# Storing the expert result rows by an indirect DMA that leaves out unused rows

## What is computed

```python
def _hier_moe(h, w_rg, b_rg, w_re, b_re, w_gate, w_up, w_down):
    t = h.reshape(b * s, d)                       # 512 tokens x 1024
    g_logits = (t @ w_rg + b_rg)                  # 4 groups of 8 experts
    g_idx = jnp.argmax(g_logits, axis=-1)         # one group a token
    e_sel = ...                                   # the 8 expert logits of that group
    top_v, top_i = lax.top_k(e_sel, 2)            # two experts a token
    top_w = jax.nn.softmax(top_v, axis=-1) * g_w
    for gi in range(4):
        hg, hu = t @ w_gate[gi], t @ w_up[gi]     # 1024 -> 256, each expert
        act = jax.nn.silu(hg) * hu * combine
        out = out + act @ w_down[gi]              # 256 -> 1024
```

## Time and profile before

| | us |
|---|---|
| median of 3 runs (891.83 to 893.46) | 893.3 |
| the profiled execution, whole | 893.97 |
| its span, from first to last instruction | 892.2 |
| PE busy | 778.1 (87%) |
| DVE busy | 436.9 (49%) |
| ACT busy | 179.4 (20%) |
| POOL busy | 156.1 (18%) |

### The profile page before, as it was taken

How to read it: one execution, slowest core, us unless ns; L and a number is a source line. 1 busy time by engine, 2 the same in 40 slices (tenths; PEclk the granted TensorE clock), 3 DMA queues, 4 the chain that set the end, 5 groups by cost and what they waited for, 6 DMA issues and landing times.

```text
span 892.2 us, 9829 instructions
## 1 busy us (share of the span) xinstructions
PE 778.1 (87%) x3913; PEld 527.0 (59%) x3913; DVE 436.9 (49%) x743; ACT 179.4 (20%) x333; POOL 156.1 (18%) x74
## 2 busy tenths in 40 slices
PE   0399997799999999999999999999999989988700
PEld 0388786789887888544444688885554544544200
DVE  5999806455668888311135678362212220211138
ACT  4212323344232321000000110121111111111022
POOL 5734663220042221100000060000000000000042
PEclk9999998899999999999999999999999999999955
DMA  9523321111121132622110351807999999999562
GB/s 294 191 93 96 94 94 48 48 49 48 48 95 48 48 82 61 239 91 79 63 47 1 139 239 47 327 4 279 423 424 422 423 422 421 423 423 422 228 212 95
DMA packets 57860, 163.48 MB, mean 183 GB/s; under 512 B 14412, under 2 KB 37078, under 8 KB 45014
## 3 DMA queue, kind: packets, MB, share of 16 engines
q1 hardware_dynamic: 51744, 139.68, 41.2%
q0 software_dynamic: 3072, 12.63, 4.0%
q10 hardware_dynamic: 2998, 10.53, 2.9%
HBM read 148.15 MB, written 14.68 MB: 182 GB/s over the span
## 4 chain that ended last, share of the span: by engine, by line
PE 71%; DMA 15%; DVE 9%; issue 2%; ACT 1%; POOL 1%; SPq 1%; ACTq 0%; DVEq 0%; POOLq 0%
PE psum L744 24%; DMA ring<-in_w_exp_up_dram 11%; PE psum L1038 9%; PE psum L953 6%; PE psum L943 6%; PE psum L992 5%; PE psum L1053 3%; PE psum L934 3%; PE psum L1015 2%; DMA ring<-in_w_in_dram 2%; PE psum L1016 2%; DVE arena L1398 2%; PE psum L883 2%; DVE arena L1397 2%; PE psum L903 1%
## 5 line engine op out<-in xcount | busy, mean ns | idle before, releaser
L744 PE MATMUL psum<-ring_r 128*128 128x512 f32 (+1 forms) x768 | 213.3, 363 | 2.6 <-DVE arena L1569 1.3
L744 PEld LDWEIGHTS psum<-ring_r 128*128 128x128 f32 x768 | 139.4, 194 | 26.2 <-issue 2.4
L675 POOL TENSOR_TENSOR ring_r<-ring,ring_r 128x2048 fp32r<-128x2048 f32 x20 | 93.4, 4670 | 205.5 <-ACT ring_r L1109 205.5
L1038 PE MATMUL psum<-ring,arena 128*64 128x512 f32 x512 | 113.1, 594 | 11.5 <-DMA ring<-in_w_exp_up_dram 10.7
L1109 ACT COPY arena<-psum 128x512 f32<-128x512 f32 (+3 forms) x102 | 57.5, 582 | 290.8 <-PE psum L960 139.8
L744 PE MATMUL psum<-arena_r,ring_r 128*128 128x512 f32 x256 | 100.5, 392 | 0.0
L1038 PEld LDWEIGHTS psum<-ring,arena 128*64 128x64 f32 x512 | 40.2, 137 | 82.7 <-issue 81.8
L1824 DVE SCALAR_TENSOR_TENSOR arena<-arena,psum 128x256 f32<-128x256 f32 x16 | 9.9, 621 | 120.5 <-ACT arena L1291 120.5
L707 POOL DMA_INDIRECT ring<-y_rows,rowsU x8 | 9.1, 1132 | 328.5 <-ACT arena L1109 326.4
L1015 PE MATMUL psum<-arena_r 128*128 128x256 f32 x256 | 65.3, 293 | 0.0
L1016 PE MATMUL psum<-arena_r 128*128 128x256 f32 x256 | 62.5, 282 | 0.0
(11 more groups left out here) (242 smaller groups left out, 956.8 us busy)
## 6 DMA issues: line engine op xcount, KB each, us to landing
ring<-in_w_exp_gate_dram SPq DMA_DIRECT2D x32, 1024.0 KB, 17.3
ring<-in_w_exp_up_dram SPq DMA_DIRECT2D x32, 1024.0 KB, 19.5
ring<-in_w_exp_down_dram SPq DMA_DIRECT2D x32, 1024.0 KB, 19.4
ring<-in_w_in_dram SPq DMA_DIRECT2D x18, 1024.0 KB, 5.1
y_rows<-arena ACTq DMA_DIRECT2D x16, 512.0 KB, 8.0
y_rows<-arena POOLq DMA_DIRECT2D x4, 1024.0 KB, 7.2
ring<-in_w_out_ssd_dram SPq DMA_DIRECT2D x4, 1024.0 KB, 7.3
ring<-in_w_out_dram SPq DMA_DIRECT2D x4, 1024.0 KB, 11.1
```

What stands on the lines that cost most here:

```text
L675: g.tensor_tensor(lo, ring[:, SLOT_OF[seq]], hi.bitcast(F32), ALU.subtract).then_inc(s_w_lo, 1)
L744: t = mm(o, a, b, start=(first and j == 0), stop=(last and j == 2))
L1038: t = mm(psum[sides[half], parity, :], xgT[buf][:, k, c:c + CAP], ring[:, s:s + 2, k, :], start=(k == 0), stop=(k == KD - 1))
```

## The change

Three things are changed.

1. The store of a pair's results moves from ACT (direct DMA) to POOL, which issues an indirect DMA for each of the 16 pairs. It takes the row number of each partition from a column of `storeU`; a used row has its old number, an unused one a number beyond the buffer, and rows beyond the buffer are left out (`oob_is_err=False`). The further pairs in the loop keep ACT's direct store, with a wait for it behind.
2. DVE computes `storeU`: two small compares where the counts are, and three small operations after the last embedding tile. POOL makes two more small index tables.
3. All 3072 rows of `y_rows` are zeroed early, by twelve DMAs of 1 MB in place of four, at the same place.

```diff
-ZERO_DMAS = (ROWS - NE * CAP) // P // 2
+ZERO_DMAS = ROWS // P // 2
...
-            zview_y = y_dram[NE * CAP:ROWS].rearrange("(p r) n -> p r n", p=P)
+            zview_y = y_dram.rearrange("(p r) n -> p r n", p=P)
             for r in range(0, zview_y.shape[1], 2):
                 pool.dma_start(zview_y[:, r:r + 2, :], zt).then_inc(s_zeroed, 16)
...
+            g.iota(row_id, pattern=[[2 * CAP, PAIRS]], base=0, channel_multiplier=1,
+                   allow_small_or_imprecise_dtypes=True).then_inc(s_iota_c, 1)
+            g.iota(row_of, pattern=[[-CAP, 2]], base=0, channel_multiplier=1,
+                   allow_small_or_imprecise_dtypes=True).then_inc(s_iota_c, 1)
             pool.wait_ge(s_pe_yT, NT)
...
+            pool.wait_ge(s_store_ready, 1)
+            for p in range(PAIRS):
+                pool.wait_ge(s_y_act, p + 1)
+                pool.wait_ge(s_y_dve, p + 1)
+                g.indirect_dma_start(
+                    out=y_dram, out_offset=bass.IndirectOffsetOnAxis(ap=storeU[:, p:p + 1], axis=0), in_=eout[:, p % 2, :],
+                    in_offset=None, bounds_check=ROWS - 1, oob_is_err=False).then_inc(y_st[p % 2], 16)
             pool.wait_ge(s_rows_ready, 2)
             pool.wait_ge(s_blocks_stored, 1)
...
                 copy(eout[:, u % 2, 0:512], psum[:, 4, :]).then_inc(s_y_act, 1)
-                act.wait_ge(s_y_act, p + 1)
-                act.wait_ge(s_y_dve, p + 1)
-                act.dma_start(y_dram[bass.ds(p * 2 * CAP, 2 * CAP)], eout[:, u % 2, :]).then_inc(y_st[u % 2], 16)
...
-            act.wait_ge(y_st[0], pairs * 16 + 16 * (PAIRS // 2))
+            act.wait_ge(y_st[0], 16 * (PAIRS // 2))
             act.wait_ge(y_st[1], 16 * (PAIRS // 2))
...
+            dve.wait_ge(s_iota_c, 3)
+            for half in range(2):
+                q = slice(half * CAP, (half + 1) * CAP)
+                ins = v.tensor_tensor(store_f[q], count[q, half:NE:2], row_of[q, half:half + 1].broadcast_to([CAP, PAIRS]),
+                                      ALU.is_gt)
+                link(ins)
...
             for n in range(4 * NT - RANKS_AFTER, 4 * NT):
                 ple_out(n)
+            link(v.tensor_scalar(store_f, store_f, -float(4 * ROWS), float(4 * ROWS), ALU.mult, ALU.add))
+            link(v.tensor_tensor(store_f, store_f, row_id, ALU.add))
+            v.tensor_copy(storeU[:, :], store_f).then_inc(s_store_ready, 1)
             dve.wait_ge(s_pe_pl, 4 * NT)
             tokens_rows(1, 1, None, 1, 4 * CAP)
```

More of the change, by code:

```diff
@@ L109 @@
 RING = SLOTS * SLOT
-ARENA = 28600
+ARENA = 28512
 RANKS_AFTER = 2
@@ L356, in block_kernel @@
         sums = shaped(region(4 * NT), "p (i n) -> p i n", i=NT, n=4)
+        row_id = at(region(PAIRS), PAIRS)
+        row_of = at(region(2), 2)
+        store_f = at(region(PAIRS), PAIRS)
+        storeU = ctx.enter_context(nc.sbuf_tensor("storeU", [P, PAIRS], U32))
         rowsU = ctx.enter_context(nc.sbuf_tensor("rowsU", [P, 2 * NT], U32))
@@ L400, in block_kernel @@
         s_iota_c = sem("iota_c")
+        s_store_ready = sem("store_ready")
         s_hT_read = sem("hT_read")
@@ L409, in block_kernel @@
         s_mix_read = sem("mix_read")
+        s_more_stored = sem("more_stored")
         s_mix_ready = sem("mix_ready")
@@ L1328, in _ @@
                     act_copy(p, 0)
-                    out_copy(p, j * 16 + 16 * (PAIRS // 2), 0)
+                    out_copy(p, 16 * (PAIRS // 2), 0)
+                    act.wait_ge(s_y_act, p + 1)
+                    act.wait_ge(s_y_dve, p + 1)
+                    act.dma_start(y_dram[bass.ds(p * 2 * CAP, 2 * CAP)], eout[:, 0, :]).then_inc(s_more_stored, 16)
+                    act.wait_ge(s_more_stored, j * 16 + 16)
+                    copy(rv[10], rv[8])
                 act.nop()
-            act.wait_ge(y_st[0], pairs * 16 + 16 * (PAIRS // 2))
+            act.wait_ge(y_st[0], 16 * (PAIRS // 2))
             act.wait_ge(y_st[1], 16 * (PAIRS // 2))
@@ L1802, in h1_rest @@
                 v.tensor_tensor(h_lo[:, i], h1[:, i], h_hi[i].bitcast(F32), ALU.subtract).then_inc(s_h1_lo, 1)
-            dve.wait_ge(s_iota_c, 1)
             tokens_rows(0, 0, None, None, 4 * CAP)
@@ L1844, in _ @@
                     hidden(j + PAIRS, 0)
-                    out_half(j + PAIRS, j * 16 + 16 * (PAIRS // 2), 0)
+                    out_half(j + PAIRS, 16 * (PAIRS // 2), 0)
+                    dve.wait_ge(s_more_stored, j * 16 + 16)
+                    v.tensor_copy(rv[11], rv[8])
                 dve.nop()
```

## The result

The changed kernel takes 882.4 us (881.1 to 883.7), the kernel before 892.6 us (891.5 to 893.5) beside it on the same chip. The ratio is 0.9887, 95% interval 0.9870 to 0.9904. That is 10.2 us less, where the prediction said 4.7 less. The prediction started from a median before of 893.3, which is 892.6 here; 0.7 us of the distance is that. The profiled execution took 883.66 us with a span of 881.9, against 893.97 and 892.2 before, 10.3 us less in the span.

What follows compares the result with a forecast made beforehand. The prediction took the DMA engines to bound the expert stage from pair 7 on; -5.1 (stores) + 0.4 (end) + 0 (zeroing, small work) = -4.7 us gave 889.3 for the profiled execution, 888.6 as median, range 884.0 to 894.3.

Steps and rivals of the forecast that it cites:

- What bounds the kernel: Expert stage: DMA engines bound it, TensorE's lead used up by pair 7; stores of pairs 0 to 13 take 17.4 us.
- The price of a row: Stores in the expert stage: one 4096 B row costs its DMA engine 0.155 us.
- Which engine has which row: Stores: four neighbouring rows from each 32 of a half, as the Trainium skill's descriptor swizzle states; fullest engine carries 79 of 112.
- the middle of the bounds: Store gain: bounds 0 and 9.2 us, middle 4.6; the 5.1 us split was taken as nearest to it.
- From rows to time: Expert stage: fullest engine by store rows decides when weights land; 33 rows fewer at 0.155 us gain 5.1 us.
- GB/s as a witness: 616 to 829 us: rate falls from 422 to 413 GB/s if the split is right, stays at 422 with an even spread.
- The stores on POOL: Expert stage: moving the stores to idle POOL costs 0, at 1.11 us an issue; queue cost bounds 0 and 1.3 us.
- The end of the stage: After the last copies: path goes from ACT's loop to POOL's last store, +0.4 us, bounds -0.4 and +2.0.
- Gathers and adds: After the expert stage: the gathers and all behind them stay the same.
- Zeroing and small operations: Early zeroing and small DVE and POOL work: hidden, 0; bounds 4 us for zeroing, 1 us for small work without cover.
- The range: Whole kernel, 8 in 10: 884.0 to 894.3 us, taking in the forecast, most of the even spread and eight neighbours.
- The even spread: Rival on the stores: rows spread evenly or nearly so over engines, -7.1 to -9.2 us, 884.5 to 886.6 us; chance 0.25.

Runs made afterwards that it cites:

- even_rows: Changed kernel, but only rows of even partitions stored, 64 of 128 in every pair: 882.5 us, ratio to the kernel before 0.9896, pair 0 to pair 15 225.0 us.
- low_half: Changed kernel, but only rows of partitions 0 to 63 stored in every pair: 891.5 us, ratio to the kernel before 0.9994.
- quarter16: Changed kernel, but only rows of partitions whose number modulo 32 is under 16 stored: 890.8 us, ratio to the kernel before 0.9993.
- block4: Changed kernel, but only rows of partitions whose number modulo 8 is under 4 stored: 892.4 us, ratio to the kernel before 1.0004.
- the runs with one engine's rows: Changed kernel storing only partitions 0-3 and 32-35, 8-11 and 40-43, 16-19 and 48-51, or 24-27 and 56-59: 888.8, 888.8, 888.5, 890.3 us.
- upper_half: Changed kernel, but only rows of partitions 64 to 127 stored in every pair: 892.1 us, ratio to the kernel before 0.9993.
- all_rows: Changed kernel, but POOL's indirect DMA stores every row of every pair, used or not: 891.0 us, ratio to the kernel before 1.0001.
- zero12_only: Kernel before with the early zeroing alone, twelve DMAs in place of four: 891.7 us, ratio to the kernel before 0.9998.

## Why the prediction was right or wrong

**What bounds the kernel.** Right. The stage is bound by the DMA engines from pair 7 on, only the stores of pairs 0 to 13 count, and up to 600 us nothing moved.

**The price of a row.** Right: 0.155 predicted; 0.152 from `even_rows`; 0.155 from the packets, which follow each other by that when they have 4 KB.

**Which engine has which row.** Right, chosen among four from the middle of the bounds, and borne out by `low_half`, `quarter16`, `block4` and the runs with one engine's rows. The middle of the bounds was no reason for it, and that it pointed to the right one was luck; what spoke for it was the page that the prediction names. The fullest engine by store rows has 79 of 112 left.

**From rows to time.** This is the step that failed. "A weight load has landed only when the slowest of its 16 engines is through" is right, but the prediction took it that the slowest before and the slowest after are each the one with the most store rows, as if all had the same other work. Before, all have 112 rows, and yet the slowest are 3.0 us behind the engine of partitions 0 to 3 and 32 to 35 (233.6 against 230.6). One of the slowest has partitions 24 to 27 and 56 to 59, and by the chains it gets two instruction fetches, which would make the 3.0 us (1.5 of them come at the ninth fetch; the rest is argued). These partitions are late ones of a half: of its 112 rows, 41 are used. The change takes 71 rows x 0.155 = 11.0 us from it, and it is out of the way, at 233.6 - 11.0 = 222.6.

Which engine is the slowest afterwards isn't shown; two fit. One is the engine of partitions 0 to 3 and 32 to 35, which never fetches and keeps 79 rows: 230.6 - 33 x 0.155 = 225.5 us. The gain would then be 5.1 us of rows, as forecast, and 3.0 us of surplus that the old slowest engine had and the new one hasn't: 8.1. The other is the second engine with two fetches, which has 112 rows before as well. It must be in the upper half (`upper_half`, 233.9), and if `quarter16` (234.0), which leaves out partitions 24 to 27, is late by the same engine, it is one of the four with partitions 64 to 79 and 96 to 111. These keep 56 to 67 rows: 224.9 to 226.6 us, and the gain would be 7.0 to 8.7 us of rows of an engine that is late before and after. Measured: 225.7, and 7.7 between the two profiled executions (233.4 - 225.7). In both cases the step fails in the same way: an engine's store rows alone don't tell how late it is. The same arithmetic gives `even_rows`, where an engine with two fetches stays the slowest: 233.6 - 56 x 0.155 = 224.9, measured 225.0. The levels were measured with masks; in the trace of the changed kernel, where the engines have unlike rows, the chains could not be kept apart well enough.

The row that gives it away stands in the view from which the earlier trace rows are: the line of q8, 0.3% of the time of 16 engines. An average of 0.3% is 10.5 us of engine time in 218 us, and if it falls on single engines, with what it costs the next packet it's 1.5 to 3 us for the one on which it falls. It was passed over as small.

**GB/s as a witness.** Wrong. The prediction wanted 413 GB/s with this split, since fuller engines hold the others up; it stayed at 420. And `low_half` and `upper_half`, which gained nothing, show full DMA engines in the first window and nearly so in the second (columns as in the earlier trace rows; first `low_half`, then `upper_half`; behind them the weight loads of the kernel before):

```profile
616.00:703.00 87.00, 87.00 (x490) 44.52 (x488) 22.12 (x30) 14.49 (x30) 4.96 (x6) 1.00 1.01 419
703.00:820.00 117.00, 107.06 (x582) 55.38 (x580) 20.58 (x29) 16.91 (x35) 7.66 (x8) 0.99 1.01 412
```

```profile
616.00:703.00 87.00, 86.58 (x486) 44.12 (x484) 22.13 (x30) 14.52 (x30) 5.67 (x6) 1.00 1.01 417
703.00:820.00 117.00, 108.06 (x594) 56.18 (x592) 20.59 (x29) 16.94 (x35) 7.74 (x8) 1.00 1.00 410
```

```profile
ring<-in_w_exp_gate_dram SPq DMA_DIRECT2D x28, 1024.0 KB, 17.4
ring<-in_w_exp_up_dram SPq DMA_DIRECT2D x28, 1024.0 KB, 19.5
```

The relieved engines don't stand still, they run ahead. In the kernel before a weight load takes 2.5 us of the engines' time and lands 17 to 20 us after its issue (the two rows above, issues from 600 to 836 us: count, KB, median us to landing), so some seven loads are queued, and an engine with fewer rows works on the next ones while TensorE waits for the slowest. Only when the lead is used up, late in the stage, does the rate fall by some 3%. A full DMA share and a full rate don't show that the engines are even.

**The stores on POOL.** Price 0 right (`all_rows`). POOL takes 0.98 us an issue, forecast 1.1.

**The end of the stage.** Forecast +0.4, measured -0.7, a miss of 1.1 us, and 0.3 outside its own bounds of -0.4 and +2.0. It is no scatter: the time from the copies' end to the first gather is 6.0 in `zero12_only` as well, and 4.8 to 5.4 in all kernels that store by POOL. The mechanism was right: ACT is through its loop at 842.8 and the path goes over to the store (the chain above). The term that was mis-sized is its landing. It was given the 4.4 us of the fastest gather; it took 3.3 (min of the landings of line 717), little more than ACT's direct store with 2.6:

```profile
DMA to landing us min/median/max: 3.3/8.0/8.6
```

The nearer row was the same transfer on the other queue, not the other transfer on the same queue. The store was issued 0.85 us after the copies' end (839.50 to 840.35), forecast 0.9.

**Gathers and adds.** Forecast unchanged, measured -0.6 us, which is within the scatter of this part (18.0 to 18.8 us).

**Zeroing and small operations.** 0 forecast, 0 found (`zero12_only`, `all_rows`). The zeroes lasted until 69 us, forecast 68, and the late weight load landed at 71.3, forecast 70.6 at worst.

**The range.** The even spread at 884.5 to 886.6 was taken for the best that could happen, so the range stopped at 884.0. With all 9.2 us of the upper bound and the end at its own best, -0.4, it would have been 893.3 - 9.6 = 883.7, still above the 882.4 measured. The bound itself was sound for the stage (7.7 is below 9.2). Of the 5.6 us between the 889.3 forecast for the profiled execution and the 883.7 it took, 2.6 are the stretch, 1.1 the end, and 1.8 the start of pair 0 and the gathers, which are scatter. What the range lacked is the upper side: it was drawn as if all engines were alike but for their rows.

**Would an even spread of the rows do better still?** `even_rows` has fewer rows on the fullest engine than the changed kernel (56 to 79) and is only 0.8 us shorter in the stretch, which fits an engine with two fetches as the bound. Dealing the used rows out evenly, 53 to an engine, would by that bring 225.7 - (233.6 - 59 x 0.155) = 1.2 us, an estimate at the edge of what is measurable; it was not run.

## What to carry to other kernels

Where a transfer is complete only when all DMA engines are through, work out the load of each engine, not of all together, and put in everything that goes over the engines: one packet of a queue with 0.3% of the time cost its engine 1.5 us here, and by the chains one engine had two. A change that takes bytes off single engines can bring less than its share of the bytes (nothing, with the wrong half) or more, if it relieves the engine that was late for another reason. And neither the DMA share nor the GB/s tells: with deep queues the light engines run ahead, and both stay full.

## What the hardware showed beside that

- An instruction fetch (by the numbers TensorE's) is a 16 KB packet on one DMA engine. In the full stage it takes 0.9 to 1.1 us (a load's packet of 8 KB takes 0.31), and the engine's next packet of 8 KB takes 0.77 to 0.86. In the chains of the kernel before, eight of the engines take turns.
- An indirect store with row numbers beyond the buffer sends a 4 B packet of 9 ns for each dropped row (945 such packets for 945 rows).
- A direct DMA over 64 partitions used all 16 engines (stretch shorter by 8.8 us), an indirect one over 128 with 64 dropped did not (0).
- The last indirect store, 103 rows of 4 KB with nothing beside it, landed after 3.3 us, the direct one of 128 rows after 2.6.
